# Two transformer-like blocks on one core: the attention's second half of rows divided one step earlier, and both low parts of it ahead of a weight block

## The reference, cut to what matters

```
y_a = sliding_window_attention(q_a, k_a, v_a, sinks)        # p / (sum(p) + exp(sink - m)), times v
h_m = mlstm_chunkwise(q_m, k_m, v_m, i_pre, f_pre)          # num / max(|den|, exp(-m_t))
y_m = sigmoid(o_m) * head_layer_norm(h_m, mlstm_norm_w)     # mean and variance over each head's 128 columns
merged = sigmoid(g_a) * (y_a @ w_branch_attn) + sigmoid(g_m) * (y_m @ w_branch_mlstm)
mix = merged @ w_out
x = x + gate_m * rms_norm(mix, g_post_mix)
```

## Time and profile before

| what | value |
|---|---|
| median of three runs | 801.05 us (800.26 to 801.48) |
| the profiled execution, one of them | 801.48 us, of which 799.2 us are the span of the profile |
| PE busy | 764.7 us, 96% of the span |
| DVE busy | 627.4 us, 79% |
| ACT busy | 385.1 us, 48% |
| POOL busy | 41.5 us, 5% |

### The profile page before, as it was taken

The page is one execution under the profiler, slowest core; times in us unless marked ns, Lnnn a source line. Parts: engine busy times, 40 slices in busy tenths (PEclk is TensorE's granted clock), DMA queues, the critical chain, the costliest instruction groups (busy, mean ns, idle before and its releaser), DMA issues.

```text
span 799.2 us, 15838 instructions
## 1 busy us (share of the span) xinstructions
PE 764.7 (96%) x6610; PEld 697.6 (87%) x6610; DVE 627.4 (79%) x811; ACT 385.1 (48%) x551; POOL 41.5 (5%) x61
## 2 busy tenths in 40 slices
PE   4999999989999999999999999999999999999996
PEld 3798999989789999998878987989778999999874
DVE  5869989989988887886869899886697688555447
ACT  3367733745364544443445875532225454445340
POOL 0124000000010000000002000050010000000000
PEclk9999999999999999998999999999999999999999
DMA  9997867764749999987973644401265589565621
GB/s 343 313 323 222 291 205 227 237 222 158 232 137 337 320 348 313 334 312 256 362 244 113 221 132 129 164 4 29 94 224 163 155 289 341 179 192 190 203 82 52
DMA packets 98069, 173.68 MB, mean 217 GB/s; under 512 B 7767, under 2 KB 55230, under 8 KB 97998
## 3 DMA queue, kind: packets, MB, share of 16 engines
q1 hardware_dynamic: 95678, 166.62, 62.3%
q0 software_dynamic: 1872, 5.86, 2.5%
q10 hardware_dynamic: 448, 0.19, 0.1%
HBM read 171.60 MB, written 1.05 MB: 216 GB/s over the span
## 4 chain that ended last, share of the span: by engine, by line
PE 73%; DVE 19%; issue 3%; ACT 2%; DMA 2%; DVEq 0%; SPq 0%; ACTq 0%
PE bank L2129 13%; PE bank L2130 13%; PE bank L2131 13%; PE bank L2402 5%; PE bank L2403 5%; PE bank L2404 5%; DVE wlo L473 3%; DVE acc L500 3%; PE bank L2104 2%; PE bank L2106 2%; PE bank L2105 2%; DMA raw<-in_w_ada 2%; PE bank L2564 1%; PE bank L2045 1%; DVE arena L1523 1%
## 5 line engine op out<-in xcount | busy, mean ns | idle before, releaser
L473 DVE TENSOR_TENSOR wlo<-raw,whi 128x1024 fp32r<-128x1024 f32 (+1 forms) x212 | 254.4, 1214 | 84.2 <-ACT whi L694 80.5
L694 ACT ACTIVATE whi<-raw 128x1024 fp32r<-128x1024 f32 (+1 forms) x212 | 219.9, 1051 | 201.4 <-PE bank L2131 77.1
L2129 PE MATMUL bank<-hh,whi 128*128 128x256 f32 x1016 | 283.7, 279 | 3.1 <-DVE hl L1222 2.9
L2130 PE MATMUL bank<-hl,whi 128*128 128x256 f32 x1016 | 281.2, 277 | 0.0
L2131 PE MATMUL bank<-hh,wlo 128*128 128x256 f32 x1016 | 281.2, 277 | 0.0
L2129 PEld LDWEIGHTS bank<-hh,whi 128*128 128x128 f32 x1016 | 190.8, 188 | 6.5 <-issue 5.6
L2131 PEld LDWEIGHTS bank<-hh,wlo 128*128 128x128 f32 x1016 | 191.3, 188 | 0.0
L2130 PEld LDWEIGHTS bank<-hl,whi 128*128 128x128 f32 x1016 | 190.8, 188 | 0.5 <-issue 0.5
L2402 PE MATMUL bank<-whi,ffh 128*128 128x512 f32 x168 | 66.9, 398 | 0.9 <-DVE wlo L473 0.9
L2403 PE MATMUL bank<-wlo,ffh 128*128 128x512 f32 x168 | 66.4, 395 | 0.0
L2404 PE MATMUL bank<-whi,ffl 128*128 128x512 f32 x168 | 66.3, 395 | 0.0
(11 more groups left out here) (450 smaller groups left out, 1062.3 us busy)
## 6 DMA issues: line engine op xcount, KB each, us to landing
raw<-in_w_ada SPq DMA_DIRECT2D x96, 512.0 KB, 5.3
raw<-in_w_in SPq DMA_DIRECT2D x54, 512.0 KB, 4.7
raw<-in_w_ffn_in SPq DMA_DIRECT2D x88, 256.0 KB, 3.8
raw<-in_w_ffn_gate SPq DMA_DIRECT2D x44, 256.0 KB, 4.6
raw<-in_w_ffn_up SPq DMA_DIRECT2D x44, 256.0 KB, 5.7
raw<-in_w_ffn_down SPq DMA_DIRECT2D x22, 512.0 KB, 5.3
raw<-in_w_ffn_out SPq DMA_DIRECT2D x22, 512.0 KB, 4.3
raw<-in_w_out SPq DMA_DIRECT2D x16, 512.0 KB, 4.3
```

The lines of the kernel that those rows point to most:

```text
L473: eng.tensor_tensor(lo[:, 0:nk * width], raw[:, b % RAW, 0:nk * width], hi[:, 0:nk * width].bitcast(fp), ALU.subtract)\
L694: act.activation(weight_place(g)[0][:, 0:nk * width], raw[:, b % RAW, 0:nk * width], ACT.Copy)\
L2129: mm(o, wh[:, k, c], xh[:, kk_, :], start=first, stop=False)
L2130: mm(o, wh[:, k, c], xl[:, kk_, :], start=False, stop=False)
```

## The change

Nothing is added or removed; three DVE instructions change places.

- `head_stats` takes a function that is called ahead of the last head. For half 0 that function is `divided(1)`: the division of the attention's second half of rows now stands ahead of the last pair of statistics instead of behind `head_var(0)`.
- `split_ya(1)`, the second low part, now stands directly behind `split_ya(0)`, and the first weight block of `ba1` (`prepare("ba1", slice(0, 1))`) behind both.

```
-            def head_stats(m):
+            def head_stats(m, amid=None):
...
                 for h in range(HM):
+                    if amid and h == HM - 1:
+                        amid()
                     step(dve.bn_stats(st[:, 144 + 6 * h:150 + 6 * h], intra[:, m, h, 0:128]))
                     step(dve.bn_aggr(st[:, 176 + 8 * m + 2 * h:178 + 8 * m + 2 * h], st[:, 144 + 6 * h:150 + 6 * h]))
...
             take_inter(0)
             divided(0)
-            head_stats(0)
+            head_stats(0, lambda: divided(1))
             head_var(0)
-            divided(1)
             split_ya(0)
+            split_ya(1)
             prepare("ba1", slice(0, 1))
-            split_ya(1)
             head_shift(0)
             take_inter(1)
```

## The result

The changed kernel takes 803.45 us (median of 20 runs, 799.92 to 806.82), the kernel before, timed beside it, 801.03 us (20 runs, 798.91 to 805.26). The forecast was 800.8 us and no difference. The profiled execution took 802.80 us.

The account below looks back on a forecast made before the run. PE, busy 96% of the span, was taken as the bound, losing time only in three waits on one chain. The shift's 0.28 us gain, taken from the median 801.05, gave 800.8 us; range 799.4 to 802.2.

Parts of the forecast that it names:

- The change, step by step: First block's mixer: start times worked through division, transposes, copy and low parts; `ba0` starts 0.76 us earlier.
- The shift: DVE step behind the weight block, releasing the mLSTM half: starts at 176.45 instead of 176.73, a gain of 0.28 us.
- DVE's two new waits, for `o_done` and for the copy: DVE waits before the early division (attention's end) and before the second low part: 0.17 and 0.20 us.
- the sum: Orders behind 186 us are unchanged, so the shift's 0.28 us reach the end: from 801.05 to 800.8 us.
- The end of the stretch: Up to the second transposes of `ym`: they start at 186.19 instead of 186.47, PE's wait growing from 1.37 to 1.85 us.
- the transfer: SP's `w_ada` block goes out 0.97 us later, at 176.56, with 12 us to spare; costed at nothing.
- rival C: PE's longer wait for `ym` lets its clock fall at 186 us, costing 3.44 us: 804.2 us; chance 0.08.
- a fall of the clock between 172 and 190 us: One of the signs named beforehand that would show the prediction wrong, in the stretch around the change.
- The range: Forecast, nearby rivals with the spread of three runs, and mild ends of the clock rivals: 799.4 to 802.2 us.

Follow-up runs that it names:

- the three repeats: The changed kernel, unaltered, run three times more beside the kernel before: medians 801.83, 802.11 and 802.71 us.
- e17: The changed kernel, unaltered, run again for a fourth profile: 802.71 us, ratio 1.0014 to the kernel before.
- e11: The changed kernel with 12 more idle matmuls just ahead of the first feed-forward, so it begins without a wait: 800.68 us, ratio 0.9998.
- e13: The changed kernel with 4 more idle matmuls ahead of the first feed-forward, for a shorter wait there: 801.07 us, ratio 1.0013.
- e14: The changed kernel with three empty DVE instructions ahead of the low part that releases the first feed-forward, starting it later: 802.19 us, ratio 1.0019.
- e16: The kernel before, unchanged, run again for a third profile: 800.51 us, ratio 1.0004.
- e5: The changed kernel, unaltered, run again for a second profile: 801.83 us, ratio 1.0006 to the kernel before.
- e2: The kernel before with only the second low part moved ahead of the weight block, the division left in place: 799.98 us, ratio 0.9991.
- e3: The changed kernel with 14 idle matmuls filling PE's wait for `ym`: 799.67 us, ratio 0.9994 to the kernel before.
- e6: The changed kernel with idle matmuls filling both PE waits, for the second low part and for `ym`: 802.20 us, ratio 1.0016.

## Why the prediction was wrong

**The change, step by step: right.** The transposes lost their wait, the copy's path shortened, DVE has no wait before the shift, and the wait for `ym` grew to 1.88 us (worked out: 1.85; the earlier trace rows had 1.37). In the three repeats it was 1.92 us. That the first profile comes so near is partly luck: its products `ba0` and the first block of `ba1` went at the slower pace too (8.59 us from 174.19 to 182.78, against 8.28 before), which took 0.3 us from that wait.

**The shift: a size.** From `take_inter(0)` to the shift it takes 8.99, 8.97 and 8.97 us in the profiles of before, and 8.33, 8.59, 8.45 and 8.66 in the four of the changed kernel: a gain of about 0.5, not 0.28. DVE's two new waits, for `o_done` and for the copy, did not appear in the first profile: there PE was ahead of DVE. In e17, where it was not, DVE waits 0.20 us for `o_done`. But behind the shift stands what no term has: DVE is idle for 0.59 us before `take_inter(1)` (the row of 175.93 above), where it was 0.23 before:

```profile
177.12 1.40 DVE L1446 SCALAR_TENSOR_TENSOR arena<-bank,st,arena 128x129 f32<-128x129 f32 x4 [0.23 <-DVE st L1484]
```

This stall of 0.36 is in all thirteen profiles with the early division, and in none of the seven without. What makes it is open. From `take_inter(0)` to `weigh_y(1)` it is then 17.98, 17.95, 17.95 before and 17.66, 17.91, 17.77, 17.97 after: a gain of 0.13 us in the mean where the sum has 0.28.

**The end of the stretch, and the transfer: right.** SP issued the `w_ada` block at 175.30, right behind the weight block as before (175.27), and between 187 and 236 us PE has the same three waits as before (0.6, 0.2 and 1.0 us).

**The step that failed** is the sum: "behind 186 us the orders are unchanged and all that runs there is released by this chain, so the 0.28 us reach the end". The orders are unchanged, but a time won is only kept if the work behind takes as long as before. Here it did not, twice:

- *The pace of the feed-forward run*: 1.22 us lost, in four of four profiles. Another start of that run brought the quicker pace back (e11, e13, e14), and the time of before with it in e11, though not in e13 and e14. It was no rival.
- *Low clock behind the wait for `ym`*: rival C's mechanism, at half its price, since the stretch is 3.4 us and not 8: some 1.7 us, in three of four profiles. It got a chance of 0.08. The earlier trace rows had shown that waits of 1.67 and 1.37 us left the clock at 1.00, but in that one execution; e16 is the same kernel, with the clock at 0.50 behind the wait of 1.67. A single profile was read as a threshold. The sentence of the Trainium skill that stood against the change there ("TensorE: Matmul & The Clock Gate", Why this matters for your kernels: idle gaps send the clock back) is borne out in kind: the clock fell behind waits of 1.88 and 1.92 us in three profiles, shorter gaps than the page warns of, and in e5 it did not.

The forecast had named a fall of the clock between 172 and 190 us as what would make it wrong, and it fell at 186.2. But by the runs it is the smaller of the two. At equal mean clock, where stretches of low clock drop out, the chain's -0.1 and the pace's +1.2 make 1.1 us. Measured are 1.43 over all runs, and 0.7 to 1.0 in the three repeats against their own chips; the sum lies between, so the size is not settled better than to some 0.4 us. What goes with the clock is the rest of the 1.70, 0.27 us: the mean clock of the changed kernel is 0.9903, that of before 0.9908. A stretch of 3.4 us at half speed in three executions of four would lower it by 0.0016; the kernel before has low clock too, behind the first wait, in e16 and in e2 with that part of the change.

**The range** rested on three runs that lay 1.2 us apart. Twenty runs of either kernel reach over 6 us.

**What is open.** What sets the pace: in the first feed-forward part it is there from the first matmuls on, and the length of the wait ahead of it does not decide it; no other instruction or transfer that differs was found. Why three instructions that change places 50 us ahead should turn it is not explained. Whether the change also alters how often the second block's runs go at the slower pace was not tested. Whether the division alone is worth having: its two runs give 0.9988 and 0.9996, both intervals hold 1, so no gain is shown.

## What to carry to other kernels

A gain that is handed to one wait of PE comes back at the next one, and the longer wait can cost more than it is long: ask for each wait what the clock does behind it, in several executions, not in one. Where a kernel got slower and its waits don't say why, count matmuls per 20 us at full clock in all long runs, those ahead of the change too: what differs there differs between executions, and only a stretch that is the same in each profile of a kernel can be laid to the change. A shift below a microsecond is judged only over many runs, at equal mean clock and against the same chip, since stretches of low clock move the time by several microseconds from one execution to the next.

## What the runs showed of the hardware

- Long runs of 128x256 matmuls, each with its weight load, go at one of two paces at full clock: 113.3 or 117.8 ns from start to start. In the first feed-forward part the pace was kept to the end of the run, and was the same in each profiled execution of a kernel. It can turn without a pause: in e3, from 104.2 us on, 49 matmuls at 113.3 ns are followed by 47 at 117.8. In the second block's (612 to 632 and 648 to 668 us) both paces occur in the same kernel: 113.3 and 117.8 in either stretch, in changing combinations.
- The run of the mLSTM branch, 190 to 202 us, has the two paces as well: 113.3 in the profiles of the kernel before and of the changed one, 117.8 with the division alone and with the filled waits of e3 and e6.
- Low clock that falls ahead of a wait can be paid out of it: with 176.7 to 180 us at 0.50 the wait of 1.37 us for `ym` was gone, and that execution was the quickest profiled one of the kernel before (span 794.9 us; it also lacks the low clock that the other two have at 359 us).
